# The clamps of the value products ahead of the mix of the two maps, and weight splits one per step

## The reference, cut to what matters

```python
def diff_attention(q, k, v, lam):          # q, k (B,H,2,S,d), v (B,H,S,2d)
    ...
        p = jax.nn.softmax(logits, axis=-1)
        pd = p[:, :, 0] - lam * p[:, :, 1]
        return jnp.einsum('bhqk,bhkd->bhqd', pd.astype(v.dtype), v)

yb = diff_attention(qd, kd, vd, lam)
yb = rms_norm(yb, g_subln[l], SUBLN_EPS) * (1.0 - lam_init)
yb = merge_heads(yb) * jax.nn.silu(zb)
```

## Time and profile before

| what | value |
|---|---|
| median of 3 runs | 2452.34 us (2446.66 to 2452.53) |
| profiled execution | 2451.77 us, its span 2449.7 us |
| mean granted TensorE clock | 0.974 |
| PE, DVE, ACT, POOL busy | 94%, 46%, 36%, 8% of the span |
| the 8 turns of attention | about 1473 to 2104 us of the span |
| differential turns | 1542.5 to 1621.9, 1699.9 to 1781.2, 1859.6 to 1939.0, 2015.0 to 2104 |

### The profile page before, as it was taken

How to read it: one execution, slowest core, us unless ns; L and a number is a source line. 1 busy time by engine, 2 the same in 40 slices (tenths; PEclk the granted TensorE clock), 3 DMA queues, 4 the chain that set the end, 5 groups by cost and what they waited for, 6 DMA issues and landing times. The chain is left out here.

```text
span 2449.7 us, 33964 instructions
## 1 busy us (share of the span) xinstructions
PE 2296.2 (94%) x11898; PEld 1836.2 (75%) x11898; DVE 1115.6 (46%) x3122; ACT 886.0 (36%) x2276; POOL 202.7 (8%) x315
## 2 busy tenths in 40 slices
PE   6999999999979997999989799999999999799998
PEld 5888888888858877677767687767767676688876
DVE  4355264352552114445543335665665665533342
ACT  4142241340442113545542233544444444423232
POOL 1000000000000000122110000010010100101013
PEclk9999999999989999999999899999999999899999
DMA  4111111111144213011134401111011102334322
GB/s 140 37 52 52 67 46 62 43 60 36 49 165 164 78 64 117 9 50 50 50 115 133 163 9 50 59 42 43 25 43 59 43 12 72 113 89 120 96 95 86
DMA packets 125298, 175.10 MB, mean 71 GB/s; under 512 B 7576, under 2 KB 73176, under 8 KB 123616
## 3 DMA queue, kind: packets, MB, share of 16 engines
q1 hardware_dynamic: 119088, 157.39, 19.7%
q10 hardware_dynamic: 6064, 15.84, 1.7%
HBM read 143.79 MB, written 29.42 MB: 71 GB/s over the span
## 5 line engine op out<-in xcount | busy, mean ns | idle before, releaser
L91 PE MATMUL heads_p_ps<-ret_w_second_hi_sb,ret_hT_hi_sb 128*128 128x512 f32 x384 | 150.7, 392 | 0.8 <-DVE ret_w_second_lo_sb L515 0.8
L91 PE MATMUL heads_p_ps<-ret_w_second_lo_sb,ret_hT_hi_sb 128*128 128x512 f32 x384 | 149.7, 390 | 0.0
L91 PE MATMUL heads_p_ps<-ret_w_second_hi_sb,ret_hT_lo_sb 128*128 128x512 f32 x384 | 149.4, 389 | 0.0
L91 PE MATMUL att_proj_ps<-br_w_second_hi_sb,br_hT_hi_sb 128*128 128x512 f32 x272 | 117.4, 431 | 2.6 <-DVE br_w_second_lo_sb L2169 2.6
L91 PE MATMUL att_proj_ps<-br_w_second_lo_sb,br_hT_hi_sb 128*128 128x512 f32 x272 | 106.9, 393 | 0.0
L91 PE MATMUL att_proj_ps<-br_w_second_hi_sb,br_hT_lo_sb 128*128 128x512 f32 x272 | 106.7, 392 | 0.0
L2129 ACT ACTIVATE br_x_sb<-br_x_sb,att_max_neg_sb 128x256 f32<-128x256 f32 (+7 forms) x128 | 97.8, 767 | 14.0 <-DVE att_max_neg_sb L2342 13.7
L2608 ACT ACTIVATE mrg_yT_hi_sb<-br_y_raw_sb 128x1024 fp32r<-128x1024 f32 x32 | 33.9, 1060 | 142.3 <-PE mrg_b_ps L2539 119.7
L91 PEld LDWEIGHTS heads_p_ps<-ret_w_second_hi_sb,ret_hT_hi_sb 128*128 128x128 f32 x384 | 72.0, 188 | 17.3 <-issue 2.4
L91 PEld LDWEIGHTS heads_p_ps<-ret_w_second_lo_sb,ret_hT_hi_sb 128*128 128x128 f32 x384 | 72.1, 188 | 15.6
L91 PEld LDWEIGHTS heads_p_ps<-ret_w_second_hi_sb,ret_hT_lo_sb 128*128 128x128 f32 x384 | 72.1, 188 | 15.2
(11 more groups left out here) (471 smaller groups left out, 6508.6 us busy)
## 6 DMA issues: line engine op xcount, KB each, us to landing
early_w_kv_sb<-a_w_blocks SPq DMA_DIRECT2D x28, 1024.0 KB, 5.4
all_w_block_sb<-w_turns SPq DMA_DIRECT2D x12, 2048.0 KB, 9.2
br_y_raw_sb<-branch_yT_dram SPq DMA_DIRECT2D x32, 512.0 KB, 4.2
ret_o_dram<-early_x_rows_sb ACTq DMA_DIRECT2D x32, 256.0 KB, 2.4
all_w_block_sb<-swa_turns SPq DMA_DIRECT2D x4, 2048.0 KB, 9.5
ret_out_o_rows_sb<-ret_o_dram ACTq DMA_DIRECT2D x6, 1024.0 KB, 5.2
x_dram<-early_x_rows_sb SPq DMA_DIRECT2D x12, 512.0 KB, 3.1
heads_v_sb<-x SPq DMA_DIRECT2D x8, 512.0 KB, 4.3
```

Of the source, the lines that this page charges most:

```text
L91: mm = pe.matmul(out, rows[a], w[b], start=(k == 0 and a + b == 0), stop=(k == KT - 1 and b == 1))
```

## The change

In the differential turns the two clamps of `last` move into `divide(t)`: they come after `lam_recip` and ahead of the multiply that begins the mix. In step 0 of a fox turn and in the last turn's emptying steps, where `last` is differential too, they stay where they were. The four weight slices that were split at step 6 are split one each at steps 3, 4, 5 and 6, in all turns. On ScalarE the split stands ahead of `mean_square`, where it was behind it, and on VectorE it stays at the end of the step.

```diff
+SPLIT_STEPS = {3: (0,), 4: (1,), 5: (2,), 6: (3,)}
...
-                at_least(act, proj_done, turn.tiles(-TILES if ks[0] == 0 else 0))
+                at_least(act, proj_done, turn.tiles(-TILES if ks[0] < KT // 2 else 0))
...
                     if done:
                         copy_qk(*done)
+                    if t in SPLIT_STEPS:
+                        split_high((following or GATES).next(), SPLIT_STEPS[t])
                     if last and not last[0].fox:
                         mean_square(*last)
-                    if t == TILES - 2:
-                        split_high((following or GATES).next(), range(0, 4))
...
-                def divide(t):
+                def divide(t, last):
...
                     dve.wait_ge(lamr_done, turn.number(TILES, t + 1))
+                    if last and not last[0].fox:
+                        clamp_rows(*last)
                     first, second = (probs[:, b, a, 0:(t + 1) * P] for a in range(2))
...
-                        divide(t)
+                        divide(t, last)
...
                     if last:
                         if not last[0].fox:
-                            clamp_rows(*last)
+                            if turn.fox or t == TILES:
+                                clamp_rows(*last)
                             norm_factor(*last)
                         out_rows(*last)
-                    if t == TILES - 2:
-                        split_low((following or GATES).next(), range(0, 4))
+                    if t in SPLIT_STEPS:
+                        split_low((following or GATES).next(), SPLIT_STEPS[t])
```

## The result

The changed kernel takes 2429.15 us (median of 6 runs, 2424.72 to 2430.79), the kernel before 2450.4 us (6 runs, 2446.66 to 2454.11). The ratio is 0.9911, with a 95% interval of 0.9898 to 0.9925: it is 21 us faster. The prediction was 2437, its range 2430 to 2446, so the direction was right and the gain was under-estimated. Some 2 us of its distance from 2437 come from the starting point: the prediction counted from 2452.34 us, the median of three runs of the kernel before, and that of six is 2450.4.

The account below looks back on a forecast made before the run. TensorE was taken as the bound. Three loop turns 9.9, forget-gate turns 1.2 and the last turn 4.2 sum to 15.3 us off the profiled 2451.8, 2436.5; with the median 0.6 above, 2437 us, range 2430 to 2446.

Parts of the forecast that it names:

- The 2.39 us for `vz`: Projection at the end of step 6: TensorE's 2.39 us wait goes whole, and with it the clock's fall, 1.7 us.
- The margins at steps 1 to 6: Room between value products and transposes stays with the clamps ahead: 0.4 us at step 6, 0.35 at step 5; no stall.
- The new wait: Step 7 of differential turns: TensorE's transposes wait 2.1 us for the mix, as the room is only 1.27 us.
- The step that failed: Whole kernel: TensorE, busy for 94% of the span, is the bound and only what it waits for counts.
- The last turn: In the last turn the transpose of `y` starts at 2090.7 instead of 2094.84: 4.2 us gained.
- The power held by the mix: GpSimd's power waits for VectorE's mix to end; without such blocking 3.8 us more in all.
- Rival 1: GpSimd's power is not held up by the mix: 3.8 us more gain, 2433; chance 0.18.
- The forget-gate turns' 1.2 us: Step 7 of fox turns: TensorE's 0.32 us wait for a late VectorE copy goes, 4 turns, 1.2 us.
- The transposes, taken as 0.66 us: Step 6: TensorE begins transposes at 1764.83, needs 0.66 us for them, and comes to the projection at 1765.45.
- Rival 2: The 2.1 us wait at step 7 lowers the clock: up to 1.7 us in each of four turns, 2438 to 2444; 0.20.
- Rival 3: Slices at steps 3 to 5 and thin margin delay the mix 0.3 us in some 24 steps: 2448 or more; 0.11.
- Rival 5: Step 7's reciprocal comes no later than the products, wait only 1.3 us, power free: 2428; chance 0.06.

Follow-up runs that it names:

- e2: Against the kernel before: only the splits, one slice a step at steps 3 to 6 on both engines, clamps still behind the mix; 2448.97 us, ratio 0.9997.
- e8: Against the kernel before: only ScalarE's high parts split one a step, VectorE's four low parts still at step 6, clamps behind the mix; 2450.09 us, ratio 0.9998.
- e10: The kernel before with `y` computed three times over in steps 1 to 5 of the differential turns, lengthening VectorE's work; 2460.37 us, ratio 1.0045.
- e1: Changed kernel with the four weight slices back at step 6, so the clamps ahead of the mix alone; 2436.29 us, 0.9942 of the kernel before.
- e7: Changed kernel with the clamps back behind the mix at step 7 alone of the differential turns; 2437.39 us, 0.9949 of the kernel before.
- e4: Changed kernel with the short scores in step 0 of the loop's forget-gate turns issued five times over; 2428.63 us, 0.9912 of the kernel before.
- e5: Changed kernel with step 0's short transposes in forget-gate turns put behind the projection's slices 0 to 3; 2431.4 us, 0.9924 of the kernel before.
- e12: Changed kernel with the mix done in two halves, the first transposes waiting for the first half alone; 2429.66 us, 0.9912 of the kernel before.
- e9: Changed kernel with forget-gate step 0's transposes behind projection slices 0 to 3 and low parts of slices 4 to 7 ahead of the logits; 2431.43 us, 0.9918.
- e11: Changed kernel with `y` computed three times over in steps 1 to 5 of the differential turns; 2441.6 us, 0.9970 of the kernel before.
- e3: Changed kernel with the splits a step ahead, at steps 2 to 5; 2429.74 us, 0.9916 of the kernel before.

## Why the prediction was too careful

**Right.** The 2.39 us for `vz` went, with ScalarE's copy done before TensorE came. The margins at steps 1 to 6 held: the transposes there wait for no mix, and the clamps cost 0.40 us of the 0.5 assumed. The new wait stands where it was put, at step 7, 1.66 us where 2.1 was forecast. Forecast per loop turn: 3.3 us, found 4.1 to 4.3.

**The step that failed** is the first: "TensorE is the bound and only what it waits for counts". By it the steps 2 to 5, where TensorE shows no wait, were costed at nothing, and the 2.39 us with its clock was the main gain. e2 and e8 refute the price (the wait leaves its place, 2.2 us of it come back at others, and the time stays), and e10 confirms what stands in its place: logits, exponentials, mix, clamps, squares, power, `y`, and the next logits follow each other in VectorE's order, and that sequence is the length of a step. The clamps ahead of the mix take the squares and the power out of it: 1.57 us of waiting become 0.59, 0.98 less.

With the table, the loop turn's sum, split by steps as the prediction's terms fall (2.5 us by the logits of step 7, 3.3 in all):

| part | forecast | found (before to after) |
|---|---|---|
| steps 2 to 5 | 0 | -0.66 + 0.83 - 0.26 - 0.37 = -0.46 |
| step 6 | -2.5 | -2.78 |
| step 7 | -0.8 | -1.10 |
| turn | -3.3 | -4.34 |

Of the 1.04 us by which the turn gained more, 0.46 lie in the steps priced at nothing, 0.28 in step 6 and 0.30 in step 7. The 0.46 are what is left of the clamps' effect there after three slices were moved in.

The parts can't be told off to the two edits by simple sums, since each edit works differently with the other in place. The clamps alone (e1) take 0.20, 0.59 and 0.58 us off steps 4, 5 and 6. The slices on top of them then add 0.92 to step 3, take 0.06 off step 4, add 0.22 to step 5 and take 2.20 off step 6, where e2 has 0.60, 0.60, 0.60 and 1.79: in steps 4 and 5 they fill time in which VectorE would wait for the value products. Step 3 of the changed kernel shows what a slice of ScalarE costs with the new order. It stands ahead of the squares, which start 0.86 us behind the clamp, and 0.34 in e1:

```profile
1572.05 0.29 DVE L2281 TENSOR_SCALAR att_o_clip_sb<-att_o_ps 128x128 f32<-128x128 f32 x1 [0.73 <-PE att_o_ps L1977]
1572.39 0.62 ACT L2049 ACTIVATE br_w_diff_hi_sb<-all_w_block_sb 128x512 fp32r<-128x512 f32 x1
1572.91 0.30 ACT L2108 ACTIVATE att_o_junk_sb<-att_o_clip_sb 128x128 f32<-128x128 f32 x1
1574.63 0.15 DVE L2288 TENSOR_SCALAR att_o_high_sb<-att_o_ssq_sb 128x1 f32<-128x1 f32 x1 [0.92 <-POOL att_o_pow_sb L1852]
```

The last wait is 0.92 us and in e1 0.59, 0.33 more. That is the rest of step 3's 0.92 behind the 0.60 of VectorE's slice. The prediction had it fill time in which ScalarE waits for the clamp, at no cost. The last turn follows the same pattern: in its steps 1 to 6 it gains 3.9 us (forecast 2.5), from there to the transpose of `y` 2.0 (forecast 1.7), and gives 0.6 back at its end, at half clock: 5.3 against 4.2.

**The power held by the mix** was in the forecast and is confirmed. It starts 0.3 us into the multiply-add at step 6 and ends 0.56 us after it, and lasts 1.40 us, and 1.70 at step 7, where it took 0.70 before and takes 0.70 in e7 without the mix beside it. By that the Trainium skill's rule (SBUF — State Buffer, Who interferes with whom) agrees with the traces in the order that no row of before showed: VectorE's instruction with two inputs first, GpSimd's later. Rival 1 is out. The earlier trace rows say less about this than the prediction made of them: L2342 has one tensor as input, not two. An estimate from these rows: without this contention the power would end at 1755.95, before the mix's end at 1756.09, so that up to 0.59 us in each of the steps 4 to 7 is still paid for it. A kernel with the power elsewhere was not run.

**Terms off in size.** The forget-gate turns' 1.2 us are not there: the sum of these turns is the same to 0.2 us, though the wait of 0.32 us is gone. The transposes, taken as 0.66 us, need 0.42 from their start to the projection's (1756.14 to 1756.56), since such rows overlap. By these rows (an estimate, 0.66 - 0.42) each bracket before a projection that follows them understates TensorE's idle time by some 0.24 us, which is one reason why steps 2 to 5 of before show next to no wait.

**The rivals.** Rival 2 happened as an event: in all three loop turns the clock fell after the new wait, though e1 has the same wait without the fall. But its price is some 0.2 us a turn (e4), and not the up to 1.7 that I gave it. Rival 3, the gain handed on, is what befell e5 and e12, not this change. Rival 5, the better case, gave 2428 and is nearest to the result, but by luck: the power is not free, and the wait is 1.66, not 1.3.

**The sum again.** The 15.3 us forecast stand against 19.7 in the attention:

| part | forecast | found |
|---|---|---|
| three loop turns | 9.9 | 12.8, and 1.8 for the clock at one loop's entry |
| forget-gate turns | 1.2 | -0.2 |
| last turn | 4.2 | 5.3 |
| sum | 15.3 | 19.7 |

**What stays open.** The 1.8 us are a fall of the clock at the entry of the second differential turn. The traces of before, e1, e2, e8, e9, e10 and e11 have it, those of the changed kernel and the others don't; e3, e7, e9 and e12 have one at the third. Whether it belongs to the slower sequence or to chance isn't settled, since there is one trace of each kernel. Without it the attention gains 17.9 us. Between the 19.7 and the 21 of the medians lies a microsecond or two, within the scatter ahead of the attention.

## What to carry to other kernels

An engine that is busy 46% of the time can set the pace, if what it does is a closed sequence through other engines. Before pricing a wait of the busiest engine, measure the period of each of the other engines' sequences over a few steps, and see whether their own waits (here 1.57 us or more in each of the steps 1 to 7, for squares and a 0.70 us power) lie on that period. To learn which sequence binds, add work to one of them: 0.77 us in VectorE's steps lengthened four of five, while three casts of 0.55 us each, taken out of ScalarE's step 6, changed none. Work that only moved along the binding sequence was worth nothing (e2), and a wait taken out of it counted even where a busier engine then waited (step 7). But the bound moves with each edit: once the clamps had made the sequence shorter than TensorE's work in some steps, moving the same slices into those steps was worth 5.9 us more. So test two edits apart and together.

## What the runs showed of the hardware

A GpSimd instruction on two columns took 0.70 us alone and 1.03, 1.40 and 1.70 us beside VectorE's multiply-add of 768, 896 and 1024 columns, and ended 0.56 to 0.57 us after it.

Waits of 1.66 us at TensorE were followed by 3.4 us at half clock in each loop turn of the changed kernel's trace, in one of three in e11 and in none of three in e1, at the same place of the program. Waits of 0.77 us (e4) and of 1.37 to 1.41 us (e3) there were followed by none. So these traces show no length of a wait by which the fall could be foretold.
